# Whole-chunk splits of the weights, and queries and keys against the input's head and remainder side by side

## The reference

```python
def second_block(x, positions, ...):
    for l in range(DEPTH):
        h = swiglu(rmsnorm_2(x, ffn1_pre_g[l]), ffn1_w_in[l], ffn1_w_out[l])
        x = x + 0.5 * rmsnorm_2(h, ffn1_post_g[l])
        h = hybrid_mixer(rmsnorm_2(x, mix_pre_g[l]), positions, w_mix_in[l], ...)
        x = x + rmsnorm_2(h, mix_post_g[l])
        h = swiglu(rmsnorm_2(x, ffn2_pre_g[l]), ffn2_w_in[l], ffn2_w_out[l])
        x = x + 0.5 * rmsnorm_2(h, ffn2_post_g[l])
```

```python
proj = u @ w_in                       # u: 256 x 1024
xa, ya, q, k, v, g, sb, sc, sh, gates = jnp.split(proj, cuts, axis=-1)
ret = retention(q.reshape(B, S, 4, 256), k.reshape(B, S, 4, 256), v.reshape(B, S, 4, 512), positions)
# in retention: q = rope(q), k = rope(k) * dk**-0.5; scores = q k^T * decay; out = scores v; out normalized
ob = (silu(g) * ret) @ w_ret_out
# beside it: a gated linear recurrence (LRU) on xa, its output times gelu(ya), and a short convolution
```

## Time and profile before

| | us |
|---|---|
| median of 3 runs | 2320.49 |
| lowest, highest | 2320.24, 2321.12 |
| profiled execution | 2319.79 |
| its span, first to last instruction | 2318.0 |
| TensorE busy | 2296.8 |
| VectorE busy | 1540.9 |
| ScalarE busy | 1221.5 |

### The profile page before, as it was taken

One profiled execution on the slowest core, in us unless ns is written; L12 is line 12 of the kernel. 1 busy time (PEld: TensorE's weight loads), 2 busy tenths in 40 slices (PEclk: granted clock), 3 DMA queues, 4 the chain that ended last, 5 costly groups with the idle time before them and its releaser, 6 DMA issues.

```text
span 2318.0 us, 30390 instructions
## 1 busy us (share of the span) xinstructions
PE 2296.8 (99%) x12124; PEld 1959.9 (85%) x12124; DVE 1540.9 (66%) x2019; ACT 1221.5 (53%) x1788; POOL 79.1 (3%) x134
## 2 busy tenths in 40 slices
PE   8999999999999999999999999999999999999998
PEld 6888888888888888988888888888889888888887
DVE  6867657776566667876575665665678765756664
ACT  6645446464455556755444554554567553445553
POOL 0110000100000000000000000000000000000000
PEclk9999999999999999999999999999999999999999
DMA  8437655456656555645665465565556456554652
GB/s 334 146 119 238 198 171 209 146 170 203 211 163 217 189 172 163 206 162 183 218 199 191 157 217 192 179 221 190 173 164 214 153 183 221 195 193 164 199 193 89
DMA packets 119805, 434.91 MB, mean 188 GB/s; under 512 B 13553, under 2 KB 13809, under 8 KB 119665
## 3 DMA queue, kind: packets, MB, share of 16 engines
q1 hardware_dynamic: 119664, 432.96, 56.4%
HBM read 431.86 MB, written 1.05 MB: 187 GB/s over the span
## 4 chain that ended last, share of the span: by engine, by line
PE 95%; DVE 4%; ACT 1%; issue 0%; POOL 0%; DMA 0%; DVEq 0%; POOLq 0%; ACTq 0%
PE ub L1716 21%; PE ub L1713 11%; PE ub L1684 9%; PE ub L1686 9%; PE ub L1685 9%; PE acc L1684 8%; PE acc L1685 8%; PE acc L1686 8%; PE ub L1691 1%; PE ub L1692 1%; PE ub L1693 1%; PE acc L1747 1%; DVE wlo L1020 1%; DVE work L1208 1%; PE acc L2162 0%; DVE best L1205 0%
## 5 line engine op out<-in xcount | busy, mean ns | idle before, releaser
L1020 DVE TENSOR_TENSOR wlo<-raw,whi 128x1024 fp32r<-128x1024 f32 x776 | 913.1, 1220 | 215.2 <-ACT whi L534 213.4
L534 ACT ACTIVATE whi<-raw 128x1024 fp32r<-128x1024 f32 x776 | 777.3, 1052 | 200.9 <-PE ub L1686 140.5
L1716 PE MATMUL ub<-xhl,whi 128*128 128x512 f32 x2176 | 514.6, 390 | 0.0
L1716 PEld LDWEIGHTS ub<-xhl,whi 128*128 128x128 f32 x2176 | 404.2, 188 | 82.7 <-issue 1.3
L1684 PE MATMUL acc<-whi,bhl 128*128 128x512 f32 x736 | 288.2, 392 | 0.0
L1685 PE MATMUL acc<-wlo,bhl 128*128 128x512 f32 x736 | 286.6, 389 | 0.0
L1686 PE MATMUL acc<-whi,bhl 128*128 128x512 f32 x736 | 286.5, 389 | 0.0
L1684 PE MATMUL ub<-whi,xhl 128*128 128x512 f32 (+1 forms) x704 | 275.3, 391 | 3.0 <-DVE wlo L1020 1.5
L1713 PEld LDWEIGHTS ub<-xhl,wlo 128*128 128x128 f32 x2176 | 272.0, 191 | 6.2
L1713 PE MATMUL ub<-xhl,wlo 128*128 128x256 f32 x2176 | 275.4, 283 | 0.0
L1686 PE MATMUL ub<-whi,xhl 128*128 128x512 f32 (+1 forms) x704 | 272.5, 387 | 0.0
(11 more groups left out here) (305 smaller groups left out, 2471.7 us busy)
## 6 DMA issues: line engine op xcount, KB each, us to landing
raw<-in_w SPq DMA_DIRECT2D x776, 512.0 KB, 5.0
gain<-in_gains SPq DMA_DIRECT2D x20, 512.0 KB, 7.8
tapw<-in_taps SPq DMA_DIRECT2D x16, 512.0 KB, 4.3
DEC<-in_decay SPq DMA_DIRECT2D x2, 768.0 KB, 8.1
par<-in_par SPq DMA_DIRECT2D x2, 647.0 KB, 9.4
par<-in_par SPq DMA_DIRECT2D x2, 556.0 KB, 7.2
H<-in_x SPq DMA_DIRECT2D x2, 512.0 KB, 4.5
out_h<-H SPq DMA_DIRECT2D x4, 256.0 KB, 2.6
```

The lines of the kernel that those rows point to most:

```text
L534: do(act.activation(whi[:, s % RING, c], raw[:, slot, c], ACT.Copy), counts["w_hi"])
L1020: do(dve.tensor_tensor(wlo[:, s % RING, c], raw[:, PLACES[s][0], c], whi[:, s % RING, c].bitcast(f32), ALU.subtract), counts["w_lo"])
L1716: last = pe.matmul(bank, whi[:, s % RING, n:n + P], xhl[:, kt, :, :].rearrange("p a n -> p (a n)"), start=first, stop=stop, skip_group_che ...
```

## The change

1. `pieces` decides how many halves a split takes at once. A whole chunk is now copied in one ScalarE instruction and subtracted in one VectorE instruction over 2048 columns, and `w_hi` and `w_lo` count up by two at its end. Halves stay in the first five chunks of each of 12 stages (`STAGES`: per layer the input, feed-forward and last stage of block 1, the two feed-forward layers and the mixer of block 2) and where a step asks for half a chunk. ScalarE waits for both DMAs of a chunk before a whole copy. Of 776 half copies 120 remain beside 328 whole ones; of 776 half subtractions 128 beside 324.
2. The 16 q and k chunks use `pair` (banks of slot 0 for q, 1 for k). ScalarE copies one half out (`sums_out`) in each of these steps, ahead of the sigmoids and decays; VectorE adds the other into `tS` in place (`sums`, which releases the bank by `pd`), and the two multiplications read `tS` in SBUF.
3. At k3 ScalarE waits for all eight rotations of the layer (`qk_ready`) before its next `prep`, where it waited for `xs` of the last xa chunk.

```diff
--- before.py
+++ after.py
@@ -95,6 +95,16 @@
 
 
 PLACES = places()
+STAGES = sorted([s for L in range(LAYERS) for s in (L * B1["end"] + B1[n] for n in ("inp", "ffn", "ple"))]
+                + [LAYERS * B1["end"] + n + L * len(ORDER2) for L in range(LAYERS) for n in
+                   (AT2["f1first", 0], AT2["v", 0], AT2["f2first", 0])])
+
+
+def pieces(at, upto, half_):
+
+    s, k = divmod(at, 2)
+    opening = any(first <= s < first + 5 for first in STAGES)
+    return 1 if k or opening or at + 1 > 2 * min(upto, TOTAL - 1) + half_ else 2
 FFN_AT = {(0, "f1"): 2, (0, "f2"): 3, (1, "f1"): 4, (1, "f2"): 5}
 
 P1 = dict(conv_b=0, ln_g=4, ln_b=8, pool_scale=12, conv_pw=14, pool_w=1038, end=1294)
@@ -528,11 +538,13 @@
                         s, k = divmod(n, 2)
                         if s >= RING and k == 0:
                             act.wait_ge(sem["split_free"], s - RING + 1)
-                        c = slice(k * HALF, (k + 1) * HALF)
+                        parts = pieces(at[0], upto, half_)
+                        c = slice(k * HALF, (k + parts) * HALF)
                         slot, came, _ = PLACES[s]
-                        act.wait_ge(sem[f"w_in{2 * slot + k}"], 16 * came)
-                        do(act.activation(whi[:, s % RING, c], raw[:, slot, c], ACT.Copy), counts["w_hi"])
-                        at[0] += 1
+                        for part in range(k, k + parts):
+                            act.wait_ge(sem[f"w_in{2 * slot + part}"], 16 * came)
+                        do(act.activation(whi[:, s % RING, c], raw[:, slot, c], ACT.Copy), counts["w_hi"], parts)
+                        at[0] += parts
 
                 def used(s):
                     act.wait_ge(sem["split_free"], s + 1)
@@ -939,7 +951,14 @@
                             if j >= 2:
                                 act.wait_ge(sem["xs"], 4 * L + j - 1)
                             sums_out(j, s, (0, 0, 0, 1)[j])
-                        elif (kind, j) == ("q", 0):
+                        elif kind in ("q", "k"):
+                            slot = 0 if kind == "q" else 1
+                            if j:
+                                act.wait_ge(sem["qk_ready"], 8 * L + 2 * j - 1 + slot)
+                            else:
+                                act.wait_ge(sem["xs"], 4 * L + 3 + slot)
+                            sums_out(slot, s, slot)
+                        if (kind, j) == ("q", 0):
                             sigmoids(2)
                         elif (kind, j) == ("k", 0):
                             sigmoids(3)
@@ -953,7 +972,7 @@
                         elif (kind, j) == ("k", 3):
                             nxt("root_in")
                             do(act.activation(wide(Rg), wide(Rg), ACT.Sqrt, scale=-1.0), counts["root_ready"])
-                            act.wait_ge(sem["xs"], 4 * L + 4)
+                            act.wait_ge(sem["qk_ready"], 8 * L + 8)
                         elif kind == "g":
                             hd = j // 2
                             if j % 2 == 0:
@@ -1015,11 +1034,12 @@
 
                     while at[0] <= 2 * min(upto, TOTAL - 1) + half_:
                         s, k = divmod(at[0], 2)
-                        c = slice(k * HALF, (k + 1) * HALF)
-                        dve.wait_ge(sem["w_hi"], at[0] + 1)
+                        parts = pieces(at[0], upto, half_)
+                        c = slice(k * HALF, (k + parts) * HALF)
+                        dve.wait_ge(sem["w_hi"], at[0] + parts)
                         do(dve.tensor_tensor(wlo[:, s % RING, c], raw[:, PLACES[s][0], c], whi[:, s % RING, c].bitcast(f32),
-                                             ALU.subtract), counts["w_lo"])
-                        at[0] += 1
+                                             ALU.subtract), counts["w_lo"], parts)
+                        at[0] += parts
 
                 def used(s):
                     dve.wait_ge(sem["split_free"], s + 1)
@@ -1559,11 +1579,11 @@
                                            counts["has"] if k == 3 and f % 2 else None)
                         elif kind in ("q", "k"):
                             dst, slot = (q2, 0) if kind == "q" else (k2, 1)
-                            used(s)
+                            both = units(tS[:, slot, :])
+                            sums(slot, slot, both, "pd")
                             settle()
-                            bank = units(ub[:, 2 * slot, :])
-                            do(dve.tensor_tensor(units(tX[:, 0, :]), bank, cos_sin, ALU.mult))
-                            do(dve.tensor_tensor(units(tX[:, 1, :]), bank, sin_cos, ALU.mult), counts["pd"])
+                            do(dve.tensor_tensor(units(tX[:, 0, :]), both, cos_sin, ALU.mult))
+                            do(dve.tensor_tensor(units(tX[:, 1, :]), both, sin_cos, ALU.mult))
                             settle()
                             do(dve.tensor_tensor(dst[:, 2 * j, :], tX[:, 0, 0:S], tX[:, 0, S:], ALU.subtract))
                             do(dve.tensor_tensor(dst[:, 2 * j + 1, :], tX[:, 1, 0:S], tX[:, 1, S:], ALU.add),
@@ -2223,14 +2243,7 @@
                         elif kind == "xa":
                             pair(s, (0, 0, 0, 1)[j], "xs")
                         elif kind in ("q", "k"):
-                            slot = 0 if kind == "q" else 1
-                            fill(U_[2 * slot], "pd")
-                            for f in range(2):
-                                arrive(s, f)
-                                for kt in range(KT):
-                                    last = tile(ub[:, 2 * slot, f * S:(f + 1) * S], xhl[:, kt, :, :], s, f * KT + kt,
-                                                kt == 0, kt == KT - 1)
-                            give(last)
+                            pair(s, 0 if kind == "q" else 1, "pd")
                             if j == 0:
                                 lru_gates(2 if kind == "q" else 3)
                         elif kind == "g":
```

## The result

The changed kernel takes 2332.1 us (median of 5 runs, 2331.95 to 2335.31), the kernel before 2320.7 (median of 5, 2320.24 to 2321.12). The ratio is 1.0054, with a 95% interval of 1.0042 to 1.0065: 0.5% slower. The prediction was 2332.5. The profiled execution took 2332.1 us with a span of 2330.3, 12.3 more than before.

A forecast was written before the change was run, and what follows sets the result against it. TensorE, busy 99% of the span, plus its few waits bounds the kernel. Profiled 2319.8 + 11.1 (mixer delay) + 0.4 (ya) + 0.5 (block 1 attention) = 2331.8, median 0.7 above: 2332.5 us, range 2326 to 2337.

The forecast's parts named there:

- TensorE's saving, 0.18 to 0.22 a chunk: Mixer's q/k chunks: fewer, wider matmuls shorten each; 0.21 taken, 3.3 us for 16 chunks, 1.66 per layer.
- The test that the prediction set for it: Whole kernel: TensorE's busy time should fall by about 3 us, or the claimed matmul saving is wrong.
- No gain from multiplications out of SBUF: Two multiplications after each q/k addition: reading SBUF takes 0.69 us each, the same as from PSUM.
- The rotation of k3 at 996.15: Mixer, VectorE: later split start, five additions and merged splits move the end from 992.03 to 996.15.
- Scores at 996.2, values at 1004.6, the gated values at 1014.71: Mixer after the keys: TensorE later by 3.1, 4.65, then 5.5 us at its turned products, one delay.
- VectorE without idle time from 966 to 1014: Mixer of layer 0: the changed kernel's trace should show VectorE with no idle time from about 966 to 1014.
- its own second step: Mixer, head of g3: ScalarE waits for the keys, so TensorE takes the decayed scores 4.65 us later than before.
- Lateness per layer, 5.55 and 0.2 at ya: Mixer: the one delay costs 5.55 us per layer, 11.1 in all; ya chunks add 0.2, twice.
- Attention of block 1, 0.5 (term b): Block 1: a later head copy delays turned probabilities, 0 to 0.75 us in layer 1, about 0.1 in layer 0.
- No stall in the up chunks: Feed-forward up chunks: 1.8 us of slack, less 0.87 from the merged split, so no stall at six places.
- The sum: Whole kernel: 2319.8 + 11.1 + 0.4 + 0.5 = 2331.8 us, with 0.7 more for the median, 2332.5.
- Merging on an engine that isn't saturated: Splits: merging gives VectorE 0.07 us a chunk, but the first half is ready 1.1 later there, 0.9 on ScalarE.

The follow-up runs named there:

- merge_only: The changed kernel with queries and keys as before (48 narrow matmuls, no additions, no ScalarE wait for the keys), splits merged: 2323.15 us.
- lru_alone: The kernel before with only the LRU's work moved out of VectorE's full stretch, no pairs, splits in halves: 2320.31 us.
- lru_moved_halves: The changed kernel with all splits in halves, ScalarE's wait for the keys before the first silu, and the LRU's work moved out of VectorE's full stretch: 2318.11 us.
- additions_only: The kernel before with one more, unused VectorE addition of 512 columns in each of the 16 q/k chunks: 2325.32 us.
- queries_only: The changed kernel with pairs and additions for the queries only, keys by 48 narrow matmuls as before: 2330.16 us.
- late_wait: The changed kernel with ScalarE's wait for k3's rotation moved from before the head of g3 to before the first silu: 2328.24 us.
- pair_only: The changed kernel with every split in halves as before, queries and keys still by pairs: 2329.32 us.
- lru_moved: The changed kernel, splits still merged, with the LRU's work moved and ScalarE's wait for the keys before the first silu: 2320.14 us.
- lru_moved_six: lru_moved_halves with VectorE's subtraction merged again in q3, k3, g0, g1 and g2, ScalarE's copies in halves: 2319.86 us.
- halves_in_block1: The changed kernel with the splits of block 1 in halves again, block 2 as changed: 2332.96 us.

## Why the prediction was right

- **TensorE's saving, 0.18 to 0.22 a chunk:** right. Lateness falls by 0.18 to 0.22 at each q/k chunk that doesn't wait. In the timeline k1 and q2 have their 32 wide matmuls from 960.53 to 967.81, 3.64 a chunk, against the 3.66 of the earlier trace rows:

```profile
956.69 4.00 PE L1733 MATMUL ub<-xhl,wlo 128*128 128x256 f32 x32
960.53 7.44 PE L1736 MATMUL ub<-xhl,whi 128*128 128x512 f32 x32
967.81 4.00 PE L1733 MATMUL ub<-xhl,wlo 128*128 128x256 f32 x32
```

  The test that the prediction set for it was bad: TensorE's busy time didn't fall (2296.8 before, 2297.2 after). With unchanged matmuls that number was 2299.5 in merge_only and 2297.4 in lru_alone, so it moves by nearly as much as the saving. In lru_moved_halves, which has nearly none of the waits, it was 2294.7.
- **No gain from multiplications out of SBUF:** right. The 16 of line 1585 took 692 ns each, as those from PSUM. The access overhead that the Trainium skill gives ("Perfetto Trace Analysis", Optimizing Scalar/DVE Operations), lower for SBUF, would by the prediction's estimate have taken 0.13 a chunk off; it doesn't show here.

```profile
L1585 DVE TENSOR_TENSOR tX<-tS,trig 128x512 f32<-128x512 f32 x16 | 11.1, 692 | 0.6
```

- **The rotation of k3 at 996.15:** it ended 996.62, with 0.3 of the difference from the trace's start. additions_only and queries_only show that it is the count of additions that moves it. One term is added up wrongly, and harmlessly: 1.92 - 1.06 - 0.07 is 0.79 and not "about 0.85", while the chain uses 0.87, without the 0.07, which it takes off later.
- **Scores at 996.2, values at 1004.6, the gated values at 1014.71:** 996.67, 1004.94 and 1013.83 + 1.41 = 1015.24. Their order as one growing delay, each wait the maximum so far, is borne out by late_wait: without ScalarE's wait the second disappears, the third shrinks to 0.3, and the first stays. Among its signs the prediction has VectorE without idle time from 966 to 1014, which its own second step contradicts: between the rotation at 996.15 and the remainder at 998.24 it must stand still, and it did, for 2.10.
- **Lateness per layer, 5.55 and 0.2 at ya:** 5.8 and 0.23 to 0.27.
- **Attention of block 1, 0.5 (term b):** not borne out. The changed kernel's trace has no step there, and lru_alone has one of 1.3 with the code of before. The term fits a run in which a load happens to come late, and is at most in part the change's.
- **No stall in the up chunks:** right, no step at any of them.
- **The sum:** 12.0 over the profiled execution was forecast, its span is 12.3 longer. The 0.5 of block 1 didn't come, 0.3 came at the program's start, which isn't the change's, and the mixers lost 12.0 in place of 11.5. So two misses cancel in part, and the total is by luck a little better than its parts. The price of merging, which the prediction had only as a part of the chain and at ya, is 1 us a layer by itself.
- **Merging on an engine that isn't saturated:** by the Trainium skill (the same section) breaking up may let the work end sooner where an engine that isn't saturated makes another wait. pair_only against the changed kernel (1.5 a layer), merge_only (1.1), lru_moved against lru_moved_halves (0.9) and lru_moved_six (0.8) agree with that sentence. VectorE isn't saturated over the program but full in this stretch; grouping did give its 0.07 a chunk there, and lost more where VectorE waits for a whole copy.

What stays open: why loads of block 1 come late in some traces and not in others, how much more often that costs something with merged splits, and the scatter of 0.8 to 4.1 us of all kernels, which halves_in_block1 didn't bring under 1.

## What to carry to other kernels

An average share says nothing on room: VectorE at 66% was full for 27 us before the one point where TensorE waits for it. There five additions, 3.0 us, ended 3.0 us later at the keys, and TensorE lost 2.45 us: it had 1.1 of slack at the scores and none at the transposes. Before giving work to such an engine, follow its timeline back from the next consumer to its last idle piece, and move what nobody waits for (here the LRU's products) out of that stretch first. Splitting a producer's work in halves cost 0.07 us a chunk here, and was worth 0.8 to 1.5 us a layer, since its consumer was waiting at a few places.

## What the runs showed of the hardware

One instruction over 2048 columns took 2290 ns on VectorE and 1911 on ScalarE, two over 1024 took 1219 each (2.36 us together, since they overlap) and 1050 each:

```profile
L1040 DVE TENSOR_TENSOR wlo<-raw,whi 128x2048 fp32r<-128x2048 f32 x324 | 740.8, 2290 | 343.5 <-ACT whi L546 343.4
L1040 DVE TENSOR_TENSOR wlo<-raw,whi 128x1024 fp32r<-128x1024 f32 x128 | 150.8, 1219 | 25.4 <-ACT whi L546 25.0
```

The idle time before the whole ones is 343.5 us in 324, where before all 776 halves had 215.2: VectorE waits longer for a whole copy. Most of that costs nothing; TensorE loses by merging alone only the 1.1 a layer of merge_only and what block 1 may add. Unexpected was how well separate traces repeat: the steps of lateness of layer 0 and layer 1, and of one kernel and another, agree within 0.05 us at most chunks, far below what the medians of the runs can tell. And where ScalarE waited 1.65 us for a half chunk in place of 0.19, with the code of block 1 unchanged, TensorE lost 1.3.
